# Expert layer of a decoder step: the gate product in two fp32r products, its batches over 24 slots a tile, and the samples' V rows as the moving operand

## The chip, the cores and the metric

The kernel runs on one core of one Trainium2 chip. The metric is the device time of one execution in microseconds. The kernel before takes 4426.57 us (median of 3 runs, 4424.93 to 4427.05).

## The reference

One inference step of a two-layer decoder trunk, for 512 prompt tokens and 8 sample tokens (520 together), model width 1024. Layer 0 mixes a recurrence and a latent attention, layer 1 is a convolution module. Each is followed by the same kind of expert layer, which is what the change touches:

```
q = (xb @ w_q).reshape(blk, 8, 2, 128)
s = einsum('thpd,phkd->thpk', q, sub_keys)            # 8 heads, 2 halves, 128 keys
sv, si = top_k(s, 16)                                 # per half
top_s, top_pos = top_k(all sums of the two halves, 16)
idx = i * 128 + j of the 16 picks                     # 128 x 128 experts
g = softmax(top_s)
act = gelu(einsum('thkd,td->thk', u_tab[idx], xb))
y = einsum('thk,thkd->td', g * act, v_tab[idx])
```

All of it is f32. So each token has 128 picks (8 heads of 16), each with an expert number (i, j) and a gate g, and the output is the sum of the picked rows of V, weighed by g times the GELU of the token's product with the picked row of U.

## The kernel before

The expert layer (`peer_experts`) does not gather for the prompt tokens: it computes the product of all tokens with all 16384 rows of U and lets the gates, which are zero but for the picks, choose. It does so in 128 blocks of 128 experts.

*First half, 128 slots.* In slot n TensorE forms block n of the hidden values (`hidden`, lines 1571 to 1581): x and U are each split into a rounded high part and a remainder in fp32r (a 4-byte type that TensorE multiplies in one product), and three products (low by high, high by low, high by high) over 8 chunks and two halves of 260 tokens make 48 matmuls. ScalarE rounds a loaded block to its high part (`high`, three blocks ahead) and applies the GELU of a finished block; VectorE subtracts to get the remainder (`low`, three blocks ahead); SyncE loads U five blocks ahead and stores the hidden values to memory. Every engine works its list strictly in the written order.

Into the same slots other work is laid. In slots 0 to 15 the scores and the top 16 of each half are found. Then VectorE makes the picks of one tile of 128 tokens (`select`, lines 1830 to 1897) in 13 pieces, numbered 0 to 12, of which some lie in the slots behind that slot's `low`. There are five tiles: four of the prompt, and one that holds the 8 samples, whose picks are made first. When a tile's picks are complete, TensorE transposes them (`turn_picks`, line 1583), VectorE copies them out of PSUM (line 1942), and 16 batches of 8 tokens follow, one in each slot after the tile's first four: a tile has 20 slots. For a batch VectorE makes `onej` and `onei`, 128 picks by 8 tokens by 128 numbers, by comparison of the pick's numbers with a row 0 to 127, and then multiplies `onei` by the gate (`one_hot`, lines 1922 to 1930). TensorE multiplies the two per token, in f32 (`gates`, lines 1589 to 1597), which gives the 128 x 128 map of that token's gates; ScalarE copies the maps from PSUM (`copy_gates`, line 1690), and SyncE stores 32 tokens' maps in four pieces of 512 KB, one a slot. The slots are counted by `FIND` = 16, `ONES` = 32 and `TAIL` = 112: sixteen plain slots stand before the four tiles and sixteen after them. In the code the tiles are a loop that each engine runs by itself, on VectorE three times round and a last one written out.

*Second half, 128 blocks.* The hidden values and gates come back from memory, VectorE multiplies and splits them (`gate`), and TensorE multiplies with the blocks of V, again in three fp32r products (`out`, 24 matmuls of 512 tokens).

*The samples.* Their 128 picked rows of V each are gathered (GpSimd, lines 1532 to 1536). At the very end TensorE takes, for each of 8 samples and 8 chunks of 128 outputs, 128 x 128 of V's rows as the weights and the sample's one column of gate times activation as the moving operand (lines 1656 to 1663); VectorE adds the residual (line 1995). A LayerNorm (`layer_norm`) follows, whose first matmuls are line 322 and second line 328.

What releases what in a slot: ScalarE does the batch's two `copy_gates`, then `high`, then the GELU; `high` of three blocks ahead also waits for the block before; VectorE's `low` waits for `high`; a slot's `select` pieces stand behind its `low`; the next `one_hot` stands behind them.

Of the kernel before, what the change touches and what calls it, by code (L numbers as in the profile page):

```python
# [28 lines left out]
P = 128  # L29
# [33 lines left out]
FIND, PLAIN, BATCHES = 16, 4, TT // BT  # L63
PER_TILE = PLAIN + BATCHES
ONES = FIND + 2 * BT
# [1211 lines left out]
def peer_experts(nc, k, a, layer, xh, r):  # L1277
# [7 lines left out]
    with Stage(nc, f"experts{layer}") as s:  # L1285
# [16 lines left out]
        cols = s.sb("cols", [P, 3, TT])  # L1302
        scols = s.sb("scols", [P, 3, TS])
# [5 lines left out]
        sact = s.sb("sact", [P, TS])  # L1309
# [9 lines left out]
        over = Overlay(nc, s, "over_a", 16384)  # L1319
        first = over.row()  # L1320
        onej = first.sb("onej", [P, 2, BT, NK])
        onei = first.sb("onei", [P, 2, BT, NK])
        then = over.row()
        gated = then.sb("gated", [P, TP])
        ah = then.sb("ah", [P, 2, TP], F32R)
        al = then.sb("al", [P, 2, TP], F32R)

        over = Overlay(nc, s, "over_b", 33280)
# [5 lines left out]
        rest = first.sb("rest", [TT, NT, NK])  # L1334
        top = first.sb("top", [TT, NT, TOPK])
        topi = first.sb("topi", [TT, NT, TOPK], U32)
# [3 lines left out]

        slab = k.ring
        wq = a["peer_wq"][layer]
        hidden_of = [k.ps[:, 2 * b:2 * b + 2, 0:TH] for b in range(2)]
        q_of, y_of = k.ps[:, 4:6, 0:TH], k.ps[:, 4, 0:KC * TS]
# [31 lines left out]
        cols_copied = s.sem("cols_copied")  # L1376
        one_made = s.sem("one_made")
# [8 lines left out]
        sact_ready = s.sem("sact_ready")  # L1386
        y_summed = s.sem("y_summed")
        bank_read = s.sem("bank_read")
# [7 lines left out]
        with s.block() as block:  # L1396
            @block.sync
            def _(sp):
# [66 lines left out]

                with sp.Fori(FIND // 4, ONES // 4) as i:
                    for b in range(4):
                        plain(4 * i + b, b)
                for b in range(4):
                    plain(ONES + b, b)  # L1470
                with sp.Fori(0, NP) as t:
                    first = ONES + PER_TILE * t + PLAIN
                    for v in range(PT):
                        for b in range(PT):
                            plain(first + PT * v + b, b)
                            if v:
                                store_gates(PT * t + v - 1, (v - 1) % 2, b)
                    for b in range(PT):
                        plain(first + BATCHES + b, b)
                        store_gates(PT * t + PT - 1, (PT - 1) % 2, b)  # L1480
                for n in range(TAIL + PLAIN, NK):
# [5 lines left out]
                    if n == TAIL + PLAIN:  # L1487
                        for b in range(2):
                            sp.wait_ge(g_stored[b], 16 * 4 * NQ // 2 + 64)
                    c = n - TAIL - PLAIN  # L1490
                    if c < 8:
                        load_gates(c // 4, c // 4, c % 4)
# [55 lines left out]
            def _(pe):  # L1548
# [40 lines left out]
                def gates(n, b):  # L1589

                    pe.wait_ge(one_ready, n + 1)
# [21 lines left out]
                with pe.Fori(FIND // 4, ONES // 4 - 2) as i:  # L1613
                    for b in range(4):
                        hidden(4 * i + b, b)
                turn_picks(0)
                for n in range(ONES - 8, ONES):
                    hidden(n, n)
                with pe.Fori(0, NP) as t:
                    first = ONES + PER_TILE * t  # L1620
                    for b in range(PLAIN - 1):
                        hidden(first + b, b)
                    turn_picks(t + 1)
                    hidden(first + PLAIN - 1, PLAIN - 1)
# [41 lines left out]
            def _(act_e):  # L1666
# [66 lines left out]
                for n in range(FIND, ONES):  # L1733
                    high(n + LOW, n + LOW)
                    gelu(n, n)
                    if n == FIND + 4:
                        exponentials(0)
# [489 lines left out]
```

## Time and profile before

| | before |
|---|---|
| median of 3 runs | 4426.57 us |
| the profiled execution | 4427.57 us |
| its span | 4425.5 us |
| TensorE matmul busy | 4175.6 us (94%) |
| VectorE busy | 2527.9 us (57%) |
| ScalarE busy | 1179.3 us (27%) |
| DMA, mean | 147 GB/s |

The profile is of one execution. Busy time is the share in which at least one instruction of an engine was under way. TensorE's matmuls overlap each other in the record (each is shown longer than the interval at which the next starts), so that intervals are read from start to start. An f32 matmul appears as two records, each with a weight load of its own; an fp32r matmul as one. Line numbers are those of the kernel before.

### The profile page before, as it was taken

What the parts mean: (1) busy time and instruction counts of PE and PEld (TensorE: products, weight loads), DVE (VectorE), ACT (ScalarE), POOL (GpSimd) and SP (SyncE); (2) the same over time, 40 slices, a digit from 0 to 9 for tenths busy, and PEclk for the clock granted to TensorE, in tenths of its full rate; (3) what the DMA queues carried; (4) which work ended last, traced back from release to release, by engine and by line L of the source; (5) the groups of instructions that cost most, each with busy time, mean ns of one, the idle gap of its engine ahead of it and who ended that gap; (6) DMA issues with size and microseconds to landing.
All of it is one profiled execution on the core that took longest, in us unless ns stands there. A gap on an engine that the chain in (4) does not pass through costs nothing. (4 is left out here: it accounts for less than half of the span.)

```text
span 4425.5 us, 74733 instructions
## 1 busy us (share of the span) xinstructions
PE 4175.6 (94%) x27369; PEld 3762.6 (85%) x27369; DVE 2527.9 (57%) x4678; ACT 1179.3 (27%) x1585; POOL 38.2 (1%) x43
## 2 busy tenths in 40 slices
PE   8778679999999999999998988999999999999998
PEld 8654479999999998888888567999999998888887
DVE  3742247777776435555544846787777525555553
ACT  2101132233333321121113443223333322111111
POOL 0000000000000010000000000000000001000000
PEclk9868789999999999999998989999999999999998
DMA  3026523335445565555532012334454466555551
GB/s 111 19 92 202 170 84 105 112 126 185 154 160 171 186 233 193 193 193 194 189 112 71 24 38 96 107 123 142 165 181 157 166 209 218 192 195 190 196 190 53
DMA packets 321925, 652.38 MB, mean 147 GB/s; under 512 B 26241, under 2 KB 157442, under 8 KB 321154
## 3 DMA queue, kind: packets, MB, share of 16 engines
q1 hardware_dynamic: 318978, 642.36, 43.1%
q0 software_dynamic: 2816, 8.40, 0.5%
q8 instruction: 67, 1.10, 0.1%
q14 instruction: 64, 0.52, 0.0%
HBM read 509.00 MB, written 141.53 MB: 147 GB/s over the span
## 5 line engine op out<-in xcount | busy, mean ns | idle before, releaser
L1781 DVE TENSOR_TENSOR experts_ul<-experts_u,experts_uh 128x1024 fp32r<-128x1024 f32 x512 | 627.1, 1225 | 1074.4 <-ACT experts_uh L1678 1068.0
L1578 PE MATMUL ps<-peer_x_then_r_xh,experts_ul 128*128 128x260 f32 x4096 | 1173.3, 286 | 0.0
L1579 PE MATMUL ps<-experts_over_x_xl,experts_uh 128*128 128x260 f32 x4096 | 1157.4, 283 | 0.0
L1580 PE MATMUL ps<-peer_x_then_r_xh,experts_uh 128*128 128x260 f32 x4096 | 1155.8, 282 | 0.0
L1678 ACT ACTIVATE experts_uh<-experts_u 128x1024 fp32r<-128x1024 f32 x512 | 540.8, 1057 | 1094.7 <-PE ps L1642 1085.2
L1641 PE MATMUL ps<-experts_over_a_al,experts_uh 128*128 128x512 f32 x2048 | 797.3, 389 | 0.0
L1642 PE MATMUL ps<-experts_over_a_ah,experts_uh 128*128 128x512 f32 x2048 | 797.3, 389 | 0.0
L1640 PE MATMUL ps<-experts_over_a_ah,experts_ul 128*128 128x512 f32 x2048 | 797.2, 389 | 0.0
L1579 PEld LDWEIGHTS ps<-experts_over_x_xl,experts_uh 128*128 128x128 f32 x4096 | 772.9, 189 | 0.0
L1578 PEld LDWEIGHTS ps<-peer_x_then_r_xh,experts_ul 128*128 128x128 f32 x4096 | 772.1, 189 | 0.0
L1580 PEld LDWEIGHTS ps<-peer_x_then_r_xh,experts_uh 128*128 128x128 f32 x4096 | 771.9, 188 | 0.0
L1642 PEld LDWEIGHTS ps<-experts_over_a_ah,experts_uh 128*128 128x128 f32 x2048 | 384.6, 188 | 79.7
L1641 PEld LDWEIGHTS ps<-experts_over_a_al,experts_uh 128*128 128x128 f32 x2048 | 384.5, 188 | 79.6
L1640 PEld LDWEIGHTS ps<-experts_over_a_ah,experts_ul 128*128 128x128 f32 x2048 | 384.5, 188 | 79.5
L1683 ACT ACTIVATE experts_act<-ps 128x520 f32<-128x520 f32 x256 | 154.8, 605 | 1004.7 <-PE ps L1580 1004.6
L1595 PE MATMUL ps<-experts_over_a_onei,experts_over_a_onej 128*128 128x128 f32 x2048 | 250.1, 275 | 9.7 <-DVE experts_over_a_onei L1930 9.7
L1595 PEld LDWEIGHTS ps<-experts_over_a_onei,experts_over_a_onej 128*128 128x128 f32 x2048 | 239.6, 192 | 11.3 <-issue 11.3
L1971 DVE TENSOR_TENSOR experts_over_a_al<-experts_over_a_gated,experts_over_a_ah 128x512 fp32r<-128x512 f32 x256 | 177.3, 693 | 22.2
L1558 PE MATMUL ps<-peer_x_then_r_xh,experts_over_b_slab_l 128*128 128x260 f32 x512 | 148.4, 290 | 40.8 <-DVE experts_over_x_xl L1788 34.1
L1695 ACT ACTIVATE experts_over_b_g<-ps 128x512 f32<-128x512 f32 x256 | 150.7, 598 | 122.5 <-PE ps L1595 72.0
L1965 DVE TENSOR_TENSOR experts_over_a_gated<-experts_act,experts_over_b_g 128x512 f32<-128x512 f32 x256 | 175.1, 684 | 0.5
L1930 DVE TENSOR_TENSOR experts_over_a_onei<-experts_over_a_onei,experts_cols 128x1024 f32<-128x1024 f32 x128 | 156.9, 1226 | 11.1
(342 smaller groups left out, 4770.0 us busy)
## 6 DMA issues: line engine op xcount, KB each, us to landing
experts_u<-peer_u SPq DMA_DIRECT2D x256, 512.0 KB, 3.3
experts_u<-peer_v SPq DMA_DIRECT2D x256, 512.0 KB, 3.3
hidden<-experts_act SPq DMA_DIRECT2D x256, 260.0 KB, 2.2
gates<-experts_over_b_g SPq DMA_DIRECT2D x128, 512.0 KB, 3.0
experts_over_b_g<-gates SPq DMA_DIRECT2D x128, 512.0 KB, 5.0
experts_act<-hidden SPq DMA_DIRECT2D x256, 256.0 KB, 3.6
mla_ct<-cache SPq DMA_DIRECT2D x64, 320.0 KB, 3.8
pa_ct<-cache SPq DMA_DIRECT2D x64, 320.0 KB, 3.8
```

The source lines that it names most:

```text
L1578: pe.matmul(o, ul[:, b % 4, c], xh[:, c, t], start=(c == 0), stop=False)
L1579: pe.matmul(o, uh[:, b % 4, c], xl[:, c, t], start=False, stop=False)
L1580: mm = pe.matmul(o, uh[:, b % 4, c], xh[:, c, t], start=False, stop=(c == KC - 1))
L1595: mm = pe.matmul(k.ps[:, 4 + m, e * NK:(e + 1) * NK], onej[:, b % 2, 4 * m + e], onei[:, b % 2, 4 * m + e], start=True, stop=True)
L1640: pe.matmul(k.ps[:, c, :], ul[:, b % 4, c], ah[:, b % 2], start=first, stop=False)
L1641: pe.matmul(k.ps[:, c, :], uh[:, b % 4, c], al[:, b % 2], start=False, stop=False)
L1642: mm = pe.matmul(k.ps[:, c, :], uh[:, b % 4, c], ah[:, b % 2], start=False, stop=last)
L1678: act_e.activation(uh[:, b % 4], u[:, b % 2], ACT.Copy).then_inc(high_done, 1)
L1781: v.tensor_tensor(ul[:, b % 4], u[:, b % 2], uh[:, b % 4].bitcast(F32), ALU.subtract).then_inc(split_done, 1)
L1930: v.tensor_tensor(onei[:, b % 2], onei[:, b % 2], bc(cols[:, 2, tok], 2, NK), ALU.mult).then_inc(one_ready, 1)
L1965: v.tensor_tensor(gated[:].rearrange("p (q t) -> p q t", q=NQ), act[:, b % 4, 0:TP].rearrange("p (q t) -> p q t", q=NQ), gg[:, par, :, b], ...
L1971: v.tensor_tensor(al[:, b % 2], gated[:], ah[:, b % 2].bitcast(F32), ALU.subtract).then_inc(a_ready, 1)
```

## The change

Both expert layers change in the same way.

The gate product: `onei` is single, and two further vector instructions make `one_h` and `one_l`, `onei` times the gate's rounded high part and times its remainder, as fp32r. TensorE's one f32 matmul per token becomes two fp32r matmuls that accumulate. A tile takes 24 slots instead of 20, with no plain slots ahead: two of each three slots have a batch. The pieces of `select` go, two at a time, into the slots in which VectorE makes no batch. The prompt's first tile is chosen first and the samples' last, so that 8 instead of 16 slots stand before the tiles (`ONES` = 24, `TAIL` = 120), and 8 behind. The four stores of 32 tokens' maps are issued together at the end of each six slots. The VectorE loop goes round all four tiles, each with a full set of pieces.

The samples: the picked V rows become the moving operand, 512 columns wide, and the weights are 32 columns of which the first is the sample's. Four samples go to the four groups of 32 columns of the array. Two samples' halves make 4 PSUM banks; ScalarE and VectorE copy two banks each, 16 transposes follow, and four vector instructions add the residual.

```diff
-FIND, PLAIN, BATCHES = 16, 4, TT // BT
-PER_TILE = PLAIN + BATCHES
-ONES = FIND + 2 * BT
+FIND, BATCHES = 16, TT // BT
+PER_TILE = BATCHES * 3 // 2
+ONES = FIND + 8
...
 (SyncE)
+                    for b in range(PER_TILE):
+                        plain(first + b, b)
+                        if b % 6 == 5:
+                            for c in range(4):
+                                store_gates(PT * t + b // 6, b // 6 % 2, c)
...
 (TensorE, gates)
-                            mm = pe.matmul(k.ps[:, 4 + m, e * NK:(e + 1) * NK], onej[:, b % 2, 4 * m + e], onei[:, b % 2, 4 * m + e],
-                                           start=True, stop=True)
+                            pe.matmul(o, onej[:, b % 2, at], one_h[:, b % 2, at], start=True, stop=False)
+                            mm = pe.matmul(o, onej[:, b % 2, at], one_l[:, b % 2, at], start=False, stop=True)
...
 (TensorE, tiles)
+                    turn_picks(t)
+                    with pe.Fori(0, 2) as v:
+                        for b in range(PER_TILE // 2):
+                            if b % 3:
+                                a_ = b - 1 - b // 3
+                                gates(BATCHES * t + BATCHES // 2 * v + a_, a_)
+                            hidden(first + PER_TILE // 2 * v + b, b)
...
 (ScalarE, tiles)
+                        if b % 3:
+                            a_ = b - 1 - b // 3
+                            copy_gates(BATCHES * t + a_, a_, v)
                         plain(first + b, b)
+                        if b == 10:
+                            exponentials(t + 1)
...
 (VectorE)
+                    v.tensor_tensor(onej[:, b % 2], bc(k.iota[:], 1, BT), bc(cols[:, 1, tok], 2, NK), ALU.is_equal)
+                    wait(v, one_ready, n + 1)
+                    v.tensor_tensor(onei[:], bc(k.iota[:], 1, BT), bc(cols[:, 0, tok], 2, NK), ALU.is_equal).then_inc(one_made, 1)
+                    wait(v, one_made, n + 1)
+                    v.tensor_tensor(one_h[:, b % 2], onei[:], bc(gate_h[:, tok].bitcast(F32), 2, NK), ALU.mult)
+                    v.tensor_tensor(one_l[:, b % 2], onei[:], bc(cols[:, 2, tok], 2, NK), ALU.mult).then_inc(one_ready, 1)
+
+                PIECES = {2: (0, 1), 5: (2, 3), 8: (4, 5), 11: (6, 7), 14: (8, 9), 17: (10, 11), 20: (12,)}
+
+                with v.Fori(0, NP) as t:
+                    v.wait_ge(turned, t + 1)
+                    v.tensor_copy(cols[:], turn).then_inc(cols_copied, 1)
+                    wait(v, cols_copied, t + 1)
+                    v.tensor_copy(gate_h[:], cols[:, 2]).then_inc(gate_ready, 1)
+                    wait(v, gate_ready, 2 * t + 1)
+                    v.tensor_tensor(cols[:, 2], cols[:, 2], gate_h[:].bitcast(F32), ALU.subtract).then_inc(gate_ready, 1)
+                    wait(v, gate_ready, 2 * t + 2)
+                    for b in range(PER_TILE):
+                        if (b + 1) % 3:
+                            a_ = b - b // 3
+                            one_hot(BATCHES * t + a_, BT * a_, a_)
+                        low(first + b + LOW, b + LOW)
+                        for piece in PIECES.get(b, ()):
+                            select(piece, t + 1, t + 1, chain, STEPS * (t + 1))
...
 (TensorE, samples)
-                pe.wait_ge(bank_read, 1)
-                for n in range(TS):
-                    for c in range(KC):
-                        mm = pe.matmul(y_of[:, c * TS + n:c * TS + n + 1], rows[:, n, c * P:(c + 1) * P], sact[:, n:n + 1],
-                                       start=True, stop=True)
+                pe.wait_ge(bank_read, 4)
+                for b in range(4):
+                    for g in range(4):
+                        n, half = b // 2 * 4 + g, slice(b % 2 * 512, b % 2 * 512 + 512)
+                        mm = pe.matmul(k.ps[g * 32:(g + 1) * 32, 4 + b, :], sact[:, n], rows[:, n, half], start=True, stop=True)
+                    mm.then_inc(y_summed, 1)
+                pe.wait_ge(bank_read, 8)
+                for b in range(4):
+                    if b % 2 == 0:
+                        pe.wait_ge(y_copied[b // 2], 1)
+                    for c in range(4):
+                        mm = pe.transpose(k.ps[:, b, c * P:(c + 1) * P], y_row[:, b, c * P:(c + 1) * P], k.ident[:])
...
 (ScalarE, VectorE, samples)
+                act_e.activation(y_row[:, 0:2], k.ps[:, 4:6, :], ACT.Copy).then_inc(y_copied[0], 1)
+                v.tensor_copy(y_row[:, 2:4], k.ps[:, 6:8, :]).then_inc(y_copied[1], 1)
+                v.wait_ge(y_turned, 1)
+                for b in range(4):
+                    cs, ts = slice(b % 2 * 4, b % 2 * 4 + 4), slice(TP + b // 2 * 4, TP + b // 2 * 4 + 4)
+                    v.scalar_tensor_tensor(r[:, cs, ts], k.x[:, cs, ts], ALPHA, y_turn[:, b, :, :, 0], ALU.mult, ALU.add)
```

## Rows read from the trace of the kernel before

**Rows 1.** Windows: layer 0's tiles. Stretch, its length, busy us per engine, clock, DMA

```profile
955.00:1467.00 512.00, 507.17 (x4290) 506.37 (x4289) 366.68 (x473) 184.41 (x265) 0.00 (x0) 1.00 0.47 161
```

**Rows 2.** Waits of TensorE: who, for whom, us in total, times, longest

```profile
PE ps L1595 <- DVE experts_over_a_onei L1930: 9.7, 8, 1.3
```

**Rows 3.** Timeline of TensorE, one slot with a batch: start us, duration us

```profile
1113.30 1.95 PE L1595 MATMUL ps<-experts_over_a_onei,experts_over_a_onej 128*128 128x128 f32 x16
1115.01 0.37 PE L1578 MATMUL ps<-peer_x_then_r_xh,experts_ul 128*128 128x260 f32 x1
1115.21 0.29 PE L1579 MATMUL ps<-experts_over_x_xl,experts_uh 128*128 128x260 f32 x1
...
1120.84 1.95 PE L1595 MATMUL ps<-experts_over_a_onei,experts_over_a_onej 128*128 128x128 f32 x16
```

**Rows 4.** Windows of line 1661 alone: PE busy, PEld busy, granted clock, DMA

```profile
2306.00:2310.00 4.00, 4.00 (x38) 4.00 (x38) 1.00 0.00 0
2320.00:2325.00 5.00, 5.00 (x25) 5.00 (x25) 0.50 0.00 0
```

**Rows 5.** Groups by line: the weight loads of the fp32r and f32 products

```profile
L1579 PEld LDWEIGHTS ps<-experts_over_x_xl,experts_uh 128*128 128x128 f32 x4096 | 772.9, 189 | 0.0
L1595 PEld LDWEIGHTS ps<-experts_over_a_onei,experts_over_a_onej 128*128 128x128 f32 x2048 | 239.6, 192 | 11.3 <-issue 11.3
```

**Rows 6.** Timeline, all engines, start of a tile's first batch

```profile
1101.10 0.55 DVE L1942 COPY experts_cols<-ps 128x384 f32<-128x384 f32 x1
...
1101.84 1.22 DVE L1926 TENSOR_TENSOR experts_over_a_onej<-iota,experts_cols 128x1024 f32<-128x1024 f32 x1 [0.20 <-DVE experts_cols L1942]
...
1102.98 1.22 DVE L1927 TENSOR_TENSOR experts_over_a_onei<-iota,experts_cols 128x1024 f32<-128x1024 f32 x1
...
1105.66 2.05 PE L1595 MATMUL ps<-experts_over_a_onei,experts_over_a_onej 128*128 128x128 f32 x16 [1.28 <-DVE experts_over_a_onei L1930]
```

**Rows 7.** Timeline of VectorE: `low` in the slot of rows 3

```profile
1116.87 1.23 DVE L1781 TENSOR_TENSOR experts_ul<-experts_u,experts_uh 128x1024 fp32r<-128x1024 f32 x1 [1.01 <-ACT experts_uh L1678]
```

**Rows 8.** Timeline of VectorE: loop's return, then pieces of `select`

```profile
1084.30 1.23 DVE L1781 TENSOR_TENSOR experts_ul<-experts_u,experts_uh 128x1024 fp32r<-128x1024 f32 x1 [3.05 <-issue]
1086.90 0.69 DVE L1845 TENSOR_TENSOR experts_cand<-experts_over_x_values 128x512 f32 x1 [1.38 <-issue]
...
1089.85 1.23 DVE L1781 TENSOR_TENSOR experts_ul<-experts_u,experts_uh 128x1024 fp32r<-128x1024 f32 x1 [0.18 <-DVE experts_best L1850]
...
1092.77 0.26 DVE L1855 MATCH_REPLACE8 experts_crest<-experts_best,experts_cand 128x112 f32<-128x112 f32 x1
...
1110.47 1.50 DVE L1859 MAX8 experts_best<-experts_crest 128x8 f32<-128x112 f32 x8
...
1118.01 0.09 DVE L1863 MATCH_VALUE_LOAD experts_pos<-experts_best,experts_crest 128x8 f32 x1
...
1120.38 1.22 DVE L1926 TENSOR_TENSOR experts_over_a_onej<-iota,experts_cols 128x1024 f32<-128x1024 f32 x1
...
1155.71 2.28 DVE L1838 TENSOR_TENSOR experts_pick<-experts_ra,iota 128x2048 f32<-128x2048 f32 x1
1158.18 1.22 DVE L1926 TENSOR_TENSOR experts_over_a_onej<-iota,experts_cols 128x1024 f32<-128x1024 f32 x1 [0.18 <-DVE experts_pick L1838]
```

**Rows 9.** Timeline of TensorE in the attention: a run of column-grouped f32 products

```profile
380.47 1.93 PE L994 MATMUL ps<-mla_ct,layer_wide 128*32 128x256 f32 x32
```

**Rows 10.** Groups by line, whole span: samples' product, LayerNorm's matmuls, transposes

```profile
L1661 PE MATMUL ps<-experts_sact,experts_over_x_rows 128*128 128x1 f32 x256 | 47.1, 322 | 0.0
L328 PE MATMUL ps<-ln_sq,mean_d 128*128 128x260 f32 x128 | 28.7, 383 | 0.0
L322 PE MATMUL ps<-peer_x_then_r_r,mean_d 128*128 128x260 f32 x64 | 19.3, 474 | 2.6 <-PEq L128 2.6
L1586 PE MATMUL ps<-ident,experts_ijg 128*128 128x128 f32 x30 | 4.9, 272 | 0.0
```

**Rows 11.** Timeline of VectorE: the samples' residual in layer 1

```profile
4387.51 0.22 DVE L1995 SCALAR_TENSOR_TENSOR peer_x_then_r_r<-x,ps 128x64 f32<-128x64 f32 x1 [23.82 <-PE ps L1661]
```

More of the change, by code:

```diff
@@ L1386, in peer_experts @@
         sact_ready = s.sem("sact_ready")
+        sact_cleared = s.sem("sact_cleared")
         y_summed = s.sem("y_summed")
+        y_copied = [s.sem(f"y_copied{b}") for b in range(2)]
+        y_turned = s.sem("y_turned")
         bank_read = s.sem("bank_read")
@@ L1464, in plain @@
                     store(n, b)
[L1466 to L1470, printed above, removed]
-                with sp.Fori(0, NP) as t:
[L1472 to L1481, printed above, removed]
+                for n in range(FIND, ONES):
+                    plain(n, n)
+                with sp.Fori(0, NP) as t:
+                    first = ONES + PER_TILE * t
+                    for b in range(PER_TILE):
[3 more added lines that the diff above has]
+                                store_gates(PT * t + b // 6, b // 6 % 2, c)
+                for n in range(TAIL, NK):
                     if n + LOAD < NK:
@@ L1612, in _ @@
                     hidden(b, b)
[L1613 to L1617, printed above, removed]
+                for n in range(FIND, ONES):
                     hidden(n, n)
@@ L1620, in _ @@
                     first = ONES + PER_TILE * t
[L1621 to L1624, printed above, removed]
-                    with pe.Fori(0, BATCHES // 4) as v:
-                        for b in range(4):
-                            gates(BATCHES * t + 4 * v + b, b)
-                            hidden(first + PLAIN + 4 * v + b, b)
+                    turn_picks(t)
[5 more added lines that the diff above has]
+                            hidden(first + PER_TILE // 2 * v + b, b)
+                turn_picks(NP)
                 for n in range(TAIL, NK):
@@ L1731, in exponentials @@
                     act_e.activation(expd[:], expd[:], ACT.Exp).then_inc(exped, 1)
[L1733 to L1737, printed above, removed]
-                    if n == FIND + 12:
-                        exponentials(1)
                 def plain(n, b):
@@ L1743, in plain @@
                     gelu(n, b)
[L1745 to L1760 removed]
+                for n in range(FIND, ONES):
+                    plain(n, n)
+                    if n == FIND + 4:
+                        exponentials(0)
+                with act_e.Fori(0, NP) as t:
+                    first = ONES + PER_TILE * t
+                    for b in range(PER_TILE):
+                        v = b // 6
+                        if b % 6 == 1:
+                            act_e.wait_ge(g_stored[v % 2], 64 * (2 * t + v // 2) + 64)
+                        if b % 3:
+                            a_ = b - 1 - b // 3
+                            copy_gates(BATCHES * t + a_, a_, v)
+                        plain(first + b, b)
+                        if b == 10:
+                            exponentials(t + 1)
                 for n in range(TAIL, NK):
@@ L1784, in _ @@
                 v.sem_inc(score_free, 1)
+                v.sem_inc(one_ready, 1)
                 slab_low(0, 0)
```

102 lines of the change are left out of this document (37 added, 65 removed).

## The prediction

> **What bounds the kernel now.** I read the windows first. In layer 0's tiles the matmul engine is busy 507 of 512 us at full granted clock, VectorE 367, ScalarE 184, and the DMA engines are 0.47 busy [rows 1]. So TensorE sets the pace, and what a change of it saves there comes out at the end one for one. The waits come second: TensorE waits for the batches' one-hot arrays 9.7 us in 8 times, once at the start of each of 8 tiles, about 1.2 us each, and nowhere else in a tile [rows 2]. Third the timeline of a slot, for what a batch costs: 16 records from 1113.30 to 1115.01, 1.71 us, 0.107 us each; the first hidden matmul behind them takes 0.20 us, and the other 47 take 5.63, 0.120 each; the slot is 7.54 us [rows 3]. A plain slot is thus 48 x 0.120 = 5.75. Last the end of a layer, where TensorE works alone: the samples' product takes 47.1 us in both layers, 23.6 each, with nothing beside it [rows 10, 11].
>
> **The gate product.** 16 f32 records of 128 columns become 16 fp32r matmuls of 128 columns. No fp32r matmul narrower than 260 columns is in the trace, so the price is bounded. The streaming of 128 columns at 2.4 GHz is 0.053, and the 260-column product shows 0.120 for 0.108, 0.012 over its stream: 0.065 if only the stream counts. But each product brings a weight load. The fp32r load's record is as long as the f32 one's, 189 against 192 ns [rows 5], and what a row of loads costs with hardly a stream behind it is seen in the samples' product of one column: 38 records in 4 us at full clock, 0.105, and 25 in 5 us at half clock, 0.200, which halves to 0.100 [rows 4]. I take 0.100. The batch is then 1.60, and the 0.08 of the first hidden matmul (change of type) goes: slot 7.35, 0.19 less, x 128 batches = **-24 us** (0.105 would make it -14). Upper ends: 0.120, if the interval of the 260-column product is that of its loads: 16 x 0.120 + 5.75 = 7.67, +17; and four cycles a column, the f32 rate, 0.213: 16 x 0.213 + 5.75 = 9.16, +207.
>
> The Trainium skill (TensorE: Matmul & The Clock Gate, Weight-path perf modes) says that weights load four chunks at once where there are 128 of them and the type is not FP32, with no gain for fp32. The rows speak for the FP32 side: equal load records. By the fast side the product would cost its stream alone, which is the first rival below. The same page (Back-to-back issue gap) gives about 81 ns a product for pairs of load and 128 columns; by that the batch is 1.30 and the term -62 instead of -24. No row here shows it.
>
> **VectorE's extra product and the order of its work.** 128 more instructions of 1.14 us from start to start [rows 6] are 146 us of work. VectorE has 145 us idle per layer in the tiles [rows 1], so by busy time they cost nothing. But it works in order, and the pieces now stand two at a time behind a `low` that is released late. Take a slot with a batch that starts at S on TensorE, of the kind whose VectorE part has pieces (b = 2, 5, 8, ...). `low` began at S + 3.57 there [rows 3, 7]: GELU, the batch's two copies and `high` go before it on ScalarE. The next instruction starts 1.14 later, S + 4.7, and S + 4.6 with the shorter batch. Then come the pieces, P, and only then the `one_hot` that the slot after next needs: 3.82 us from its start to TensorE's [rows 6] plus one more instruction, 4.96. It is ready at S + 9.6 + P. TensorE is there at S + 1.60 + 2 x 5.75 = S + 13.1. It waits P - 3.5.
>
> The pieces, start to next start [rows 8]: piece 0 2.95 (1086.90 to 1089.85); pieces 1 and 2 2.0 each (1090.99, which is 1089.85 + 1.14, to 1093.03); piece 3 1.7 (1.50 and a semaphore); piece 4 2.37; pieces 7 to 11 2.47 each (1155.71 to 1158.18 shows one); pieces 5 and 6 have eight and four small instructions and are put at 1.9 and 1.3, estimates under piece 4; piece 12, one wide and three short, 3.2. The pairs: 4.95, 3.7, 4.3, 3.8, 4.94, 4.94, and 3.2 alone. Waits 1.45, 0.2, 0.8, 0.3, 1.45, 1.45, 0: 5.6 us a tile, x 8 = **+45 us**. Before, single pieces stood between batches and no such wait is in [rows 2]. Nothing absorbs it: once late, TensorE's later slots are late too, and VectorE gets ahead again only by the next group of three. The second batch of a group has slack (ready 1.14 + 4.96 = 6.1 after the first, needed after 7.35).
>
> **The start of a tile.** The three transposes now stand one slot before the first batch. From the copy of the picks to TensorE's start were 4.56 us [rows 6]; two short instructions with their semaphores (about 0.9, an estimate from the 0.74 between the copy and the next) and the extra product make it 6.6, and with about 0.6 for transposes and their landing the batch is ready 7.2 behind the first transpose, TensorE 0.3 + 5.75: a wait of 1.1, as the 1.2 before. The loop's return is new there: VectorE stood 3.05 us after it and 1.38 again after its first instruction, both put down to issue [rows 8]. The first part lies in VectorE's idle time (its `low` ends at S + 4.7, the slot at S + 7.35); the second falls into the chain: 3 returns x 2 layers x 1.4 = **+9 us** (0 to 27).
>
> Four stores at once and gates' first loads in 8 slots instead of 16: covered by U being loaded five blocks ahead and the DMA engines being half idle; without that cover 2 MB at the 161 GB/s of [rows 1] are 13 us a layer, up to +26. ScalarE's work per slot falls. I take 0.
>
> **The samples.** New: 16 f32 products of 512 columns, 32 records. Column-grouped f32 products of 256 columns ran 32 records in 1.93 us [rows 9], 0.060 each where 256 columns by [rows 3] would be 0.214 one after the other. So 32 records of 512 take 3.9, and 0.3 to land; VectorE's copy of 1024 columns about 1.3 (a 1024-column pass is 1.22 [rows 6]); the first eight transposes lie under it, the second eight cost 8 x 4.9 / 30 = 1.3 [rows 10]; four short vector instructions at 0.22 [rows 11] 0.9. In all 7.7 against 23.6 + 0.2: 16.1 x 2 = **-32 us**. If the groups did not overlap: 32 x 0.428 = 13.7 instead of 3.9, and -13. The first LayerNorm matmuls behind take 19.3 / 2 = 9.65 us where the same number at line 328 takes 28.7 / 4 = 7.2 [rows 10], because the clock fell to half in the one-column product [rows 4]. With full-width streams it may stay up: 0 to -5; I take **-2**.
>
> **Sum.** -24 + 45 + 9 - 32 - 2 = -4 us against the profiled execution of 4427.6: 4423.6. The median shown is 1.0 below that execution: 4422.6. I say 4422.
>
> **Rivals.**
> 1. *The fp32r product costs its stream only*, 0.065: batch 1.04, slot 6.79, -96 instead of -24; the waits grow a little (+8, ScalarE's copies bind). Total -68: 4358. For it: the array has nothing else to do; against it: [rows 4, 5].
> 2. *No wait behind the pairs*: VectorE's busy time is under 85% of a tile (24 x 1.14 + 16 x 4.8 + 30 + 3 = 137 of 164 us). Then -49: 4377. Against it: the order above leaves VectorE idle first and late afterwards.
> 3. *Slower: the load sets 0.120 a product.* Then the product gains nothing, +17 instead of -24, and the waits outweigh the samples' gain: +37: 4464. For it: 260 columns take 0.012 over their stream, and loads stand between all of them. It decides from about 0.107 a product (16 x 0.107 gives a term of -10 and a total of +10).
> 4. *Narrow fp32r at the f32 rate*: +207 instead of -24, +227: 4654. No row for it, none excludes it.
> 5. *The column groups don't overlap* (other weights and sources than in [rows 9]): +15: 4441.
>
> **Chances.** Forecast 0.52; rival 1 0.14; rival 2 0.11; rival 3 0.12; rival 4 0.06; rival 5 0.05. A measurement tells 0.2%, 9 us, from no change. Within the forecast the load (0.100 or 0.105: 10 us), the returns (0 to 27), pieces 5 and 6, and the LayerNorm's clock make 4400 to 4445, which leaves 0.17 faster, 0.22 same and 0.13 slower. Rivals 1 and 2 are faster (0.25), rivals 3 to 5 slower (0.23, with 0.03 of it same at their near ends). Faster 0.42, same 0.25, slower 0.33. The range takes in rivals 2, 3 and 5 and leaves out 1 and 4: 4368 to 4466.
>
> **What would show it.** The interval of the gate product, start to start: 0.100, or 0.065, or 0.120. TensorE waiting for the last `one_hot` product about 56 times (7 a tile) rather than 8, with about 1.4 us behind pairs (0,1), (8,9) and (10,11) and nearly none behind 12. First batches of tiles 1 to 3 waiting about 2.5. From the last V block to the samples' residual under 9 us. It is wrong if TensorE's waits in the tiles stay near 10 us in all, or if the product is outside 0.095 to 0.11.

## The result, and the profile after

The changed kernel takes 4476.25 us (median of 4 runs, 4473.70 to 4484.80), the kernel before beside it 4425.75 us (4 runs, 4423.59 to 4427.05). The ratio is 1.0115, with a 95% interval of 1.0102 to 1.0128: slower by 50 us. The forecast was 4422 us and its range ended at 4466.

The profiled execution took 4473.7 us, with a span of 4471.9, 46.4 more than the kernel before's 4425.5. The head of the page after, and its groups by line of the second half of a layer (the product of the gated activations with the V blocks) and of the gate product. Columns: busy us, mean ns of one, idle time before and who ended it.

```profile
span 4471.9 us, 75067 instructions
PE 4182.7 (94%) x27209; PEld 3715.9 (83%) x27209; DVE 2675.4 (60%) x4832; ACT 1182.5 (26%) x1587; POOL 39.1 (1%) x43
...
L1641 PE MATMUL ps<-experts_over_a_ah,experts_uh 128*128 128x512 f32 x2048 | 810.0, 396 | 0.0
L1639 PE MATMUL ps<-experts_over_a_ah,experts_ul 128*128 128x512 f32 x2048 | 810.0, 395 | 0.0
L1640 PE MATMUL ps<-experts_over_a_al,experts_uh 128*128 128x512 f32 x2048 | 810.0, 395 | 0.0
...
L1599 PE MATMUL ps<-experts_over_a_one_h,experts_over_a_onej 128*128 128x128 f32 x1024 | 234.4, 275 | 42.1 <-DVE experts_over_a_one_l L1924 42.1
L1599 PEld LDWEIGHTS ps<-experts_over_a_one_h,experts_over_a_onej 128*128 128x128 f32 x1024 | 196.0, 191 | 53.5 <-issue 53.5
```

The windows of layer 0's tiles and the waits of TensorE answer to [rows 1, 2]:

```profile
955.00:1467.00 512.00, 496.21 (x4151) 491.93 (x4150) 386.24 (x530) 173.58 (x245) 0.00 (x0) 1.00 0.49 157
```

```profile
PE ps L1599 <- DVE experts_over_a_one_l L1924: 42.1, 48, 1.3
```

TensorE is 11 us less busy in these 512, at the same full clock, and VectorE 20 us busier. The waits for the one-hot arrays went from 9.7 us in 8 times to 42.1 in 48.

The timeline of TensorE, one batch with its wait, answers to [rows 3] (start us, duration us):

```profile
963.00 0.28 PE L1583 MATMUL ps<-peer_x_then_r_xh,experts_uh 128*128 128x260 f32 x1
963.69 0.32 PE L1599 MATMUL ps<-experts_over_a_one_h,experts_over_a_onej 128*128 128x128 f32 x1 [0.41 <-DVE experts_over_a_one_l L1924]
963.85 0.28 PE L1600 MATMUL ps<-experts_over_a_one_l,experts_over_a_onej 128*128 128x128 f32 x1
963.96 0.27 PE L1599 MATMUL ps<-experts_over_a_one_h,experts_over_a_onej 128*128 128x128 f32 x1
...
965.41 0.28 PE L1600 MATMUL ps<-experts_over_a_one_l,experts_over_a_onej 128*128 128x128 f32 x1
965.52 0.33 PE L1581 MATMUL ps<-peer_x_then_r_xh,experts_ul 128*128 128x260 f32 x1
965.70 0.28 PE L1582 MATMUL ps<-experts_over_x_xl,experts_uh 128*128 128x260 f32 x1
```

The products start 0.112 us apart (the mean of all is 0.1117), not 0.100. The batch takes 1.83 us here, and its first product 0.16 (963.69 to 963.85). Of the 128 batches the 56 behind a gap, short ones counted, take 1.83 each; the other 72 take 1.73, with a first interval of 0.06. The first hidden matmul behind a batch takes 0.17 us in the mean (0.18 here) instead of 0.12, where the kernel before had 0.20 [rows 3].

The start of the samples' part in layer 1, all engines, answers to [rows 4, 10, 11]:

```profile
4429.62 3.64 PE L1661 MATMUL ps<-experts_over_x_rows,experts_over_a_sact 128*32 128x512 f32 x32
...
4431.67 1.02 ACT L1771 ACTIVATE experts_u<-ps 128x1024 f32<-128x1024 f32 x1 [23.23 <-PE ps L1661]
...
4433.33 1.23 DVE L1996 COPY experts_u<-ps 128x1024 f32<-128x1024 f32 x1 [2.92 <-PE ps L1661]
...
4434.61 1.09 PE L1668 MATMUL ps<-ident,experts_u 128*128 128x128 f32 x8 [0.33 <-DVE experts_u L1996]
4435.74 0.41 DVE L2000 SCALAR_TENSOR_TENSOR peer_x_then_r_r<-x,ps 128x16 f32<-128x16 f32 x4 [1.18 <-PE ps L1668]
...
4437.22 6.87 PEld L322 LDWEIGHTS ps<-peer_x_then_r_r,mean_d 128*128 128x128 f32 x32 [1.76 <-issue]
```

From the first row's start to the end of the four residual instructions it takes 6.5 us, where 7.7 were forecast. The LayerNorm's sums behind it take about 7, as they do at full clock.

Where the time of the span went, from start to start of TensorE's records:

| | before | after | difference, us |
|---|---|---|---|
| idle before batches, all 128 | 10.9 | 50.9 | +40 |
| the batches, 128 times | 1.709 | 1.778 | +9 |
| first hidden matmul behind a batch | 0.203 | 0.173 | -4 |
| the other hidden products | 119.85 ns | 119.81 ns | -1 with what lies between |
| second half, 6144 products of 512 columns | 226.68 ns | 233.33 ns | **+41** |
| samples' first product to the LayerNorm's 32nd, 2 layers | 33.3 + 34.9 | 14.5 + 14.5 | -39 |

(The waits here count the short ones too, which the page of the profile leaves out.) The sum is +46, as is the span's difference. The largest row is one that the prediction does not have: the diff has no line in the second half's product. Its records, before and after, start to start:

```profile
2099.69 0.39 PE L1641 MATMUL ps<-experts_over_a_al,experts_uh 128*128 128x512 f32 x1
2099.91 0.39 PE L1642 MATMUL ps<-experts_over_a_ah,experts_uh 128*128 128x512 f32 x1
2100.14 0.39 PE L1640 MATMUL ps<-experts_over_a_ah,experts_ul 128*128 128x512 f32 x1
2100.37 0.39 PE L1641 MATMUL ps<-experts_over_a_al,experts_uh 128*128 128x512 f32 x1
2100.59 0.39 PE L1642 MATMUL ps<-experts_over_a_ah,experts_uh 128*128 128x512 f32 x1
```

```profile
2099.63 0.40 PE L1639 MATMUL ps<-experts_over_a_ah,experts_ul 128*128 128x512 f32 x1
2099.87 0.40 PE L1640 MATMUL ps<-experts_over_a_al,experts_uh 128*128 128x512 f32 x1
2100.10 0.40 PE L1641 MATMUL ps<-experts_over_a_ah,experts_uh 128*128 128x512 f32 x1
2100.33 0.40 PE L1639 MATMUL ps<-experts_over_a_ah,experts_ul 128*128 128x512 f32 x1
2100.56 0.40 PE L1640 MATMUL ps<-experts_over_a_al,experts_uh 128*128 128x512 f32 x1
```

The group of L1640 before, whose counterpart after is L1639 above:

```profile
L1640 PE MATMUL ps<-experts_over_a_ah,experts_ul 128*128 128x512 f32 x2048 | 797.2, 389 | 0.0
```

Four intervals are 0.90 us before and 0.93 after. Weights, blocks, shapes and clock are the same. What differs is the place of `ah` and `al` in SBUF: the samples' new `sact` (1024 bytes a partition) lies ahead of them, the old one (32 bytes) is gone, and `gate_h` (512) is new. In the built programs `ah` starts at byte 169152 of the partition before, a multiple of 64, and at byte 170656 after, 32 past one. `al` lies 4096 bytes behind it in both.

### The profile page after: what moved, and what is told of

Same layout as the page of the kernel before. It is cut to its first block and busy times, and to the rows that moved or that the text cites. A ratio compares the mean times of both kernels' runs of the same rounds, so it can differ in the third digit from the quotient of the medians.

```text
span 4471.9 us, 75067 instructions
## 1 busy us (share of the span) xinstructions
PE 4182.7 (94%) x27209; PEld 3715.9 (83%) x27209; DVE 2675.4 (60%) x4832; ACT 1182.5 (26%) x1587; POOL 39.1 (1%) x43
## 5 line engine op out<-in xcount | busy, mean ns | idle before, releaser
L1641 PE MATMUL ps<-experts_over_a_ah,experts_uh 128*128 128x512 f32 x2048 | 810.0, 396 | 0.0
L1639 PE MATMUL ps<-experts_over_a_ah,experts_ul 128*128 128x512 f32 x2048 | 810.0, 395 | 0.0
L1640 PE MATMUL ps<-experts_over_a_al,experts_uh 128*128 128x512 f32 x2048 | 810.0, 395 | 0.0
L1640 PEld LDWEIGHTS ps<-experts_over_a_al,experts_uh 128*128 128x128 f32 x2048 | 384.7, 188 | 93.0
L1639 PEld LDWEIGHTS ps<-experts_over_a_ah,experts_ul 128*128 128x128 f32 x2048 | 384.7, 188 | 93.0
L1599 PE MATMUL ps<-experts_over_a_one_h,experts_over_a_onej 128*128 128x128 f32 x1024 | 234.4, 275 | 42.1 <-DVE experts_over_a_one_l L1924 42.1
L1599 PEld LDWEIGHTS ps<-experts_over_a_one_h,experts_over_a_onej 128*128 128x128 f32 x1024 | 196.0, 191 | 53.5 <-issue 53.5
L1600 PE MATMUL ps<-experts_over_a_one_l,experts_over_a_onej 128*128 128x128 f32 x1024 | 235.1, 274 | 0.0
L1600 PEld LDWEIGHTS ps<-experts_over_a_one_l,experts_over_a_onej 128*128 128x128 f32 x1024 | 196.2, 192 | 0.0
```

The lines of the kernel that those rows point to most:

```text
L1599: pe.matmul(o, onej[:, b % 2, at], one_h[:, b % 2, at], start=True, stop=False)
L1600: mm = pe.matmul(o, onej[:, b % 2, at], one_l[:, b % 2, at], start=False, stop=True)
L1639: pe.matmul(k.ps[:, c, :], ul[:, b % 4, c], ah[:, b % 2], start=first, stop=False)
L1640: pe.matmul(k.ps[:, c, :], uh[:, b % 4, c], al[:, b % 2], start=False, stop=False)
L1641: mm = pe.matmul(k.ps[:, c, :], uh[:, b % 4, c], ah[:, b % 2], start=False, stop=last)
```

## The experiments

Each ran beside the kernel before on the same chip, and ratios are to it. There were three chips: one for experiments 1 and 2, one for 3 to 5, one for 6. The kernel before had medians of 4427.4, 4428.9 and 4427.8 us there, so that a difference between experiments of different chips is good to a microsecond or two.

**1. The place of ah alone, in the kernel before** (b_ah32: 32 bytes ahead; b_ah1536: 1536 bytes, still a multiple of 64) **and in the changed kernel** (a_ah32).

```diff
 b_ah32
         gated = then.sb("gated", [P, TP])
+        then.sb("pad", [P, 8])
         ah = then.sb("ah", [P, 2, TP], F32R)
 b_ah1536
+        then.sb("pad", [P, 384])
 a_ah32
         sact = then.sb("sact", [P, TS, P // 4])
+        then.sb("pad", [P, 8])
         ah = then.sb("ah", [P, 2, TP], F32R)
```

> The kernel before with 32 bytes of padding ahead of ah and al (the moving operand of the second half), so that they start at 32 instead of 0 modulo 64 bytes, as in the changed kernel; nothing else moves. Theory A (the start of the moving operand modulo 64 bytes sets the interval of a 512-column fp32r product): the interval goes from 226.7 to 233.3 ns, 6144 products x 6.6 ns = +41 us, about 4467. Theory B (something else of the changed kernel's second half: the gates' array, the store pattern, the order of transfers): interval stays 226.7, time stays 4426.

> The kernel before with 1536 bytes of padding ahead of ah and al, so that they lie elsewhere but still at 0 modulo 64 bytes. Theory A: no change, 4426 and 226.7 ns. Theory C (the place of the moving operand relative to the weights matters, not its start modulo 64): the interval rises, up to 4467.

> The changed kernel with 32 bytes of padding ahead of ah and al alone, so that they start at 0 modulo 64 bytes again. Theory A: the interval of the second half falls from 233.3 to 226.7 ns, 4476 - 41 = 4435. Theory B: no change, 4476. The waits of the first half (6.4 us a tile) stay in both.

| | median, us (runs) | ratio, 95% | interval of 512 columns |
|---|---|---|---|
| b_ah32 | 4468.80 (4) | 1.0095, 1.0078 to 1.0112 | 233.33 ns |
| b_ah1536 | 4428.06 (10) | 1.0002, 0.9993 to 1.0012 | 226.68 ns |
| a_ah32 | 4436.34 (10) | 1.0022, 1.0013 to 1.0032 | 226.68 ns |

The group of b_ah32 and then that of a_ah32:

```profile
L1641 PE MATMUL ps<-experts_over_a_ah,experts_ul 128*128 128x512 f32 x2048 | 809.5, 395 | 0.0
```

```profile
L1640 PE MATMUL ps<-experts_over_a_ah,experts_ul 128*128 128x512 f32 x2048 | 796.7, 389 | 0.0
```

32 unused bytes make the kernel before 41 us slower, and 32 unused bytes take 40 us off the changed one; nothing else moves (the waits and the batches keep their numbers in both). A move of 1536 bytes costs nothing, so distance alone is not the cause. The size of the step is less sure than it looks: every start that ran at 226.68 ns is the same not only within 64 bytes but within 512 (the moves were 0, 1024 and 1536 bytes), and both that ran at 233.33 are 32 bytes off such a start. "A multiple of 64" is what fits below; 128, 256 or 512 would fit as well. In all the experiments that follow, `ah` has a start that ran fast, so that those on the changed kernel are compared with a_ah32.

**2. The samples' part alone, in the kernel before.** The old `sact`'s 32 bytes stay as padding and the new one lies behind `al`.

```diff
-        sact = s.sb("sact", [P, TS])
+        pad = s.sb("pad", [P, TS])
...
         al = then.sb("al", [P, 2, TP], F32R)
+        sact = then.sb("sact", [P, TS, P // 4])
...  (and the products, copies, transposes and residual of the change)
```

> The kernel before with the samples' part of the change alone (V rows stream past 32-column weights, copies, transposes); the new weights lie behind al, and the old ones' 32 bytes stay as padding, so that every other array keeps its place. If the two parts of the change add up: -19 and -20 us from the end of the last V block to the LayerNorm's first sums, 4426 - 39 = 4387. If the samples' part brought the slower second half with it: 4387 + 41 = 4428.

4386.29 us (4 runs, 4384.64 to 4388.20), ratio 0.9908 (0.9892 to 0.9925): 41 us faster, with the second half at 226.68 ns. It is the part of the change that does more than was forecast for it (-34).

**3. The order of VectorE's work.** In a_ah32, the pieces go ahead of the slot's `low`.

```diff
-                        low(first + b + LOW, b + LOW)
                         for piece in PIECES.get(b, ()):
                             select(piece, t + 1, t + 1, chain, STEPS * (t + 1))
+                        low(first + b + LOW, b + LOW)
```

> The changed kernel with ah and al back at 0 modulo 64 bytes (as a_ah32, 4436), and in VectorE's list the pieces of select ahead of the slot's low instead of behind it; the same instructions. Theory (the pieces stand behind a low that is released late): VectorE does them while it would wait for ScalarE, the batch behind is ready at about S + 11 and TensorE comes at S + 13: the waits behind pieces go (5.5 us a tile, 44 in all), 4392. Rival (VectorE is short of time in a tile, not badly ordered): its busy time is the same, so the waits stay, 4436.

4386.30 us (4 runs), ratio 0.9902 (0.9886 to 0.9919), 50 us less than a_ah32. First VectorE in the changed kernel, around the pieces of tile 0's slot 11, then in this one, then this one's waits:

```profile
969.34 1.22 DVE L1783 TENSOR_TENSOR experts_ul<-experts_u,experts_uh 128x1024 fp32r<-128x1024 f32 x1
975.71 1.23 DVE L1783 TENSOR_TENSOR experts_ul<-experts_u,experts_uh 128x1024 fp32r<-128x1024 f32 x1 [5.14 <-ACT experts_uh L1684]
976.85 0.29 DVE L1880 TENSOR_TENSOR experts_ra<-experts_ra,experts_is_b 128x128 f32<-128x128 f32 x1
...
978.04 2.30 DVE L1841 TENSOR_TENSOR experts_pick<-experts_ra,iota 128x2048 f32<-128x2048 f32 x1
980.52 1.23 DVE L1919 TENSOR_TENSOR experts_over_a_onej<-iota,experts_cols 128x1024 fp32r<-128x1024 f32 x1 [0.18 <-DVE experts_pick L1841]
...
984.13 1.22 DVE L1924 TENSOR_TENSOR experts_over_a_one_l<-experts_over_a_onei,experts_cols 128x1024 fp32r<-128x1024 f32 x1
```

```profile
967.33 2.29 DVE L1842 TENSOR_TENSOR experts_pick<-experts_ra,iota 128x2048 f32<-128x2048 f32 x1
...
973.39 1.23 DVE L1784 TENSOR_TENSOR experts_ul<-experts_u,experts_uh 128x1024 fp32r<-128x1024 f32 x1 [3.78 <-ACT experts_uh L1685]
974.54 1.22 DVE L1920 TENSOR_TENSOR experts_over_a_onej<-iota,experts_cols 128x1024 fp32r<-128x1024 f32 x1
```

```profile
PE ps L1600 <- DVE experts_over_a_one_l L1925: 5.9, 8, 0.7
```

In the changed kernel VectorE stands 5.14 us for ScalarE's high part and does the pieces afterwards, with the next batch's arrays behind them. With the pieces first they lie in that idle time, and the arrays follow `low` at once. The waits fall from 50.9 to 7.2 us, all at the tiles' first batches; the work is the same to the instruction. The batch's mean falls from 1.778 to 1.740, since 120 of the 128 now follow without a gap and take 1.73: that is another 5 us, which a wait costs beyond itself (0.10 each, 48 times).

**4. The type of the gate product.** In a_ah32, back to the f32 product of the kernel before, with three vector instructions a batch. The slots are those of the change, and the pieces stay behind `low`.

```diff
-                            pe.matmul(o, onej[:, b % 2, at], one_h[:, b % 2, at], start=True, stop=False)
-                            mm = pe.matmul(o, onej[:, b % 2, at], one_l[:, b % 2, at], start=False, stop=True)
+                            mm = pe.matmul(o, onej[:, b % 2, at], onei[:, b % 2, at], start=True, stop=True)
...
-                    v.tensor_tensor(one_h[:, b % 2], onei[:], bc(gate_h[:, tok].bitcast(F32), 2, NK), ALU.mult)
-                    v.tensor_tensor(one_l[:, b % 2], onei[:], bc(cols[:, 2, tok], 2, NK), ALU.mult).then_inc(one_ready, 1)
+                    v.tensor_tensor(onei[:, b % 2], onei[:, b % 2], bc(cols[:, 2, tok], 2, NK), ALU.mult).then_inc(one_ready, 1)
```

> The changed kernel with ah and al at 0 modulo 64 bytes, the new order of slots and pieces, but the gate product of before: one f32 product per token, three vector instructions a batch. The batch on TensorE 1.71 instead of 1.78 us (-9), and the waits behind pieces become P - 3.5 - 1.14: about 0.3 three times a tile or less, so -38. In all 4436 - 47 = 4389. If the order alone makes the waits, they stay near 5 us a tile: 4427.

4384.39 us (4 runs), ratio 0.9898 (0.9882 to 0.9915), 52 us less than a_ah32. The batch's mean is 1.721 us against 1.778, and the waits are 5.8 us in all, in an order of work that had 50.9 with the fourth instruction. The page of the profile, without the short ones:

```profile
PE ps L1598 <- DVE experts_over_a_onei L1920: 2.0, 9, 0.4
```

The split buys TensorE nothing. From a batch's start to the second hidden matmul behind it, where no gap stands ahead, both forms take 1.906 us: 1.703 and 0.203 in f32 (the kernel before, best1), 1.734 and 0.172 in fp32r (the changed kernel, a_pieces1st), and inside a batch the records start 0.1116 us apart in all four. The 1.14 us that the split adds to VectorE's part of each batch is what makes that order late. So either of two edits, this one or the one of 3, takes the same waits away.

**5. What sets the fp32r product's interval.** In a_ah32, a_mov64 streams 64 of the 128 moving columns, a_w64 loads 64 of the 128 weight columns. Each leaves out half of every token's map.

```diff
 a_mov64
-                            o, at = k.ps[:, 4 + m, e * NK:(e + 1) * NK], 4 * m + e
+                            o, at = k.ps[:, 4 + m, e * NK:e * NK + 64], 4 * m + e
-                            pe.matmul(o, onej[:, b % 2, at], one_h[:, b % 2, at], start=True, stop=False)
+                            pe.matmul(o, onej[:, b % 2, at], one_h[:, b % 2, at, 0:64], start=True, stop=False)
 a_w64
+                            o, at = k.ps[0:64, 4 + m, e * NK:(e + 1) * NK], 4 * m + e
+                            pe.matmul(o, onej[:, b % 2, at, 0:64], one_h[:, b % 2, at], start=True, stop=False)
...  (the product with one_l likewise)
```

> As a_ah32, but the two fp32r gate products take 64 of the 128 moving columns (the other half of each token's map is left out). Read from the trace: the interval between gate products. If the weight load sets it, it stays at 0.111 us; if the stream does (128 columns are 0.053), it falls by 0.027 to about 0.085.

> As a_ah32, but the weights of the two gate products are 64 of the 128 columns (half of each token's map is left out), with all 128 moving columns. If the weight load sets the interval, it falls from 0.111 to about half, 0.055 to 0.065 us; if it is the stream or a fixed cost of the product, it stays.

Each ran once. Groups of a_mov64, then of a_w64:

```profile
L1600 PE MATMUL ps<-experts_over_a_one_h,experts_over_a_onej 128*128 128x64 f32 x1024 | 231.1, 272 | 40.8 <-DVE experts_over_a_one_l L1925 40.8
L1600 PEld LDWEIGHTS ps<-experts_over_a_one_h,experts_over_a_onej 128*128 128x128 f32 x1024 | 196.5, 192 | 51.9 <-issue 51.9
...
L1582 PE MATMUL ps<-peer_x_then_r_xh,experts_ul 128*128 128x260 f32 x4096 | 1187.3, 290 | 0.0
```

```profile
L1600 PE MATMUL ps<-experts_over_a_one_h,experts_over_a_onej 128*64 128x128 f32 x1024 | 138.4, 224 | 49.7 <-DVE experts_over_a_one_l L1925 48.9
L1600 PEld LDWEIGHTS ps<-experts_over_a_one_h,experts_over_a_onej 128*64 128x64 f32 x1024 | 125.4, 135 | 61.1 <-issue 61.1
```

Half the stream leaves the interval as it is (median 0.112 us), half the load takes it to 0.060 and the batch from 1.78 to 0.98. So the load sets it: 0.112 for 128 columns. a_w64 took 4334.88 us, 101 less than a_ah32, and 128 batches of 0.80 less are 102. a_mov64 took 4465.76, 29 *more* than a_ah32 (on another chip), though it does less. The windows of the tiles say where, a_ah32 ahead of a_mov64:

```profile
955.00:1467.00 512.00, 496.21 (x4151) 491.93 (x4150) 386.27 (x534) 173.02 (x244) 0.00 (x0) 1.00 0.49 157
```

```profile
955.00:1467.00 512.00, 496.70 (x4067) 492.68 (x4066) 376.33 (x509) 170.09 (x239) 0.00 (x0) 0.98 0.48 152
```

TensorE does 84 records less in the same time at a granted clock of 0.98 instead of 1.00, and the hidden products have a mean of 290 ns instead of 284. From start to start the 12118 intervals between hidden products sum to 1502 us where a_ah32 has 1462; 527 of them are over 0.16 us, as at half clock, where a_ah32 has 170. That is the 29 us and more. Only this one run shows it, and whether it would come again is not known.

**6. What the parts make together.** best1: the changed kernel with the f32 product, the pieces first, and every array on a multiple of 64 bytes. best2 also starts the moving operands of the hidden products on such multiples, with rows of 528 columns, split 256 and 264, where rows of 520 (2080 bytes) split in two have starts of 0, 16, 32 and 48 past one.

```diff
 best1 (against the changed kernel; the f32 product as in 4, the order as in 3)
-        gate_h = s.sb("gate_h", [P, TT], F32R)
+        s.sb("pad", [P, 8])
-        over = Overlay(nc, s, "over_a", 4 * 7 * BT * NK)
+        over = Overlay(nc, s, "over_a", 16384)
 best2 (against best1)
-        xh = over.row().sb("xh", [P, KC, T], F32R)
+        xh = over.row().sb("xh", [P, KC, 528], F32R)
-                        o, t = hidden_of[b % 2][:, h], slice(h * TH, (h + 1) * TH)
+                        t = slice(256 * h, 256 if h == 0 else T)
...  (xl likewise; GELU in two instructions)
```

> The samples' part of the change, the new order of slots with the pieces ahead of the slot's low, the f32 gate product of before, and all arrays at 0 modulo 64 bytes as in the kernel before. From a_f32 (4384): its waits of 5.7 us go, the batch stays at 1.71 to 1.72 us: 4379. Against a_pieces1st (4386), which has the same order with the fp32r product, the difference should be the batch (0.02 to 0.07 us x 128 = 3 to 9) and nothing else. If the fp32r product were worth something on its own, a_pieces1st would be the faster one.

> As best1, and the first half's moving operands also start at 0 modulo 64 bytes: rows of xh and xl are 528 instead of 520 elements apart, and the two products per chunk take 256 and 264 tokens instead of 260 and 260 (in best1 they start at 0, 16, 32 or 48 modulo 64). The GELU becomes two instructions. If the 6.6 ns that 512 columns cost at 32 modulo 64 holds in proportion for 260, the interval falls from 119.8 by up to 3.4 ns: 12288 products, -42 us, 4337. If the first half is set by something else than the moving operand's read (its interval is near the 0.111 us of a weight load), nothing changes: 4379.

best1: 4377.20 us (4 runs, 4376.49 to 4378.21), ratio 0.9887 (0.9871 to 0.9904). best2: 4374.53 (4 runs, 4373.80 to 4375.69), ratio 0.9882 (0.9866 to 0.9899). The windows of best1's tiles:

```profile
955.00:1467.00 512.00, 512.00 (x4328) 512.00 (x4328) 346.01 (x493) 179.89 (x253) 0.00 (x0) 1.00 0.48 163
```

TensorE never stands: 512 of 512. It waits before no batch, which neither order had reached with four vector instructions a batch. best2's gain is 2.7 us, with hidden intervals of 119.66 ns for 119.86; so starts off a multiple of 64, which cost 6.65 ns at 512 columns, have no such price at 260. best1 is 9 us under a_pieces1st, which is that one's 7 us of waits and what they cost behind them; the type itself adds nothing (experiment 4).

## Why the prediction was wrong

It failed in one step that was missing and in one that was mis-sized; the two other large terms came out near their numbers.

*The step that is missing: the second half of a layer was taken as unchanged.* No sentence of the prediction asks where the arrays come to lie that follow the new ones in SBUF. That is +41 of the +50 us, and shown from both sides (b_ah32, a_ah32, and b_ah1536 against a rival by distance). The rows at hand could not price it, but the diff shows the shift: +1024 + 512 - 32 bytes is 1504, not a multiple of 64.

*The step that was mis-sized: the fp32r gate product at 0.100 us, forecast -24, measured 0.* (The table's +9 for the batches and -4 for the matmul behind them leave +5, which is what 48 more gaps cost the batches behind them, at 0.10 each as in experiment 3.) The load was the right cause and its price was misread. [rows 4] count the records that a window touches, also those that only reach into it, and each is longer than its interval: 38 in 4 us gave 0.105, and 25 in 5 us at half clock gave 0.200 and by halving 0.100. From start to start the same records of the kernel before are 0.1117 apart at full clock and 0.213 at half. The second misreading hid the first: the f32 batch was put at 0.107 a record [rows 3], which is 1.71 us over 16, but its records start 0.1116 apart too, and the first hidden matmul starts only 0.03 after the last of them. With 0.1117 in the prediction's own sum the slot is 16 x 0.1117 + 5.75 = 7.54, no change, as measured. So the answer lay in the trace of the kernel before. The sign that the prediction gave for being wrong here, a product outside 0.095 to 0.11, came true by a little.

Rival 3's price of 0.120 was too high, and its +37 for the total came out nearest by luck, since the slower second half made up the rest; its mechanism, a load that sets the product and takes all of its gain, is what a_w64 and a_mov64 show, and 0.112 lies past the 0.107 from which it decides. Rival 1 (0.065) falls, and so does rival 4: the narrow fp32r product of 128 columns takes 0.112, not 0.213.

The surcharge of 0.08 on the first hidden matmul behind a batch had been put down to the change of type. It stays at 0.05 with the same type on both sides, so the type explains the 0.03 between at most, and inside the batch that is lost again (1.906 us to the second hidden matmul either way).

The Trainium skill (TensorE: Matmul & The Clock Gate, Back-to-back issue gap) has about 81 ns for a pair of load and 128 columns. The fp32r pairs here measure 112, and the measurement decides.

*VectorE's order, forecast +45, measured +40, and +45 with what a gap costs the batch behind it.* This was the right reading, and the count came out too: TensorE waits 56 times, 7 a tile, short waits counted. The gaps of one tile (us):

| the batch | forecast | measured |
|---|---|---|
| tile's first | 1.1 | 0.90 |
| behind pieces 0, 1 | 1.45 | 1.44 |
| 2, 3 | 0.2 | 0.17 |
| 4, 5 | 0.8 | 0.56 |
| 6, 7 | 0.3 | 0.87 |
| 8, 9 | 1.45 | 1.18 |
| 10, 11 | 1.45 | 1.27 |
| 12 | 0 | 0 |

The wait behind pieces 6 and 7 is the one that is off, and experiment 3's rows of the changed kernel show it: `low` begins 4.38 us behind the batch at 971.33, not 3.57. ScalarE in that slot:

```profile
971.52 0.60 ACT L1689 ACTIVATE experts_act<-ps 128x520 f32<-128x520 f32 x1 [4.26 <-PE ps L1583]
972.15 1.28 ACT L1737 ACT_TABLE_LOAD   x1
973.44 0.31 ACT L1737 ACTIVATE experts_expd<-experts_expd 128x128 f32<-128x128 f32 x1
973.66 1.07 ACT L1701 ACTIVATE experts_over_b_g<-ps 128x512 f32<-128x512 f32 x2
974.61 1.06 ACT L1684 ACTIVATE experts_uh<-experts_u 128x1024 fp32r<-128x1024 f32 x1
```

The exponentials of the next tile, with a table load of 1.28 us, stand ahead of the copies and of the high part that `low` waits for. The step had left them out. That the order is the cause is shown by a_pieces1st. Rival 2, no wait because VectorE has idle time, falls: it has 126 us of it in the 512, and TensorE waits all the same.

*The loop's return, forecast +9, measured 0.* The gaps above are the same in every tile, the first included, so no return reaches TensorE. Behind a return VectorE stands 3.3 us until the transposes are done, and 0.9 where no return is ahead; the return lies in that wait, so the chain for which it was priced does not run through VectorE. Whether the 1.38 us of [rows 8] are part of it the trace does not tell.

*The samples, forecast -34 with the LayerNorm's clock, measured -39, and -41 alone.* The column groups do overlap, which settles rival 5: 32 records in 3.64 us where 3.9 were taken, and the sums behind them go at full clock (a mean of 385 ns, where the same line had 474 [rows 10]).

By the terms as measured, 0 + 45 + 0 - 39 + 41 = +47. Without the shift of `ah` it would have been about +6; a_ah32 is +8.9 over the kernel before in the same runs (4436.34 against 4427.42). The forecast had -4. About 10 us of its error are terms that it had, and that it is so little is partly luck, because they offset each other: +24 from the product, -9 from the return, -5 from the samples. The other 41 are the one that it had not.

## What to carry to other kernels

When an edit adds, drops or resizes an SBUF array, work out by how much each array behind it moves, above all wide moving operands that the edit does not name, and keep the start that it had within 64 bytes (within 512 to be safe, since only such moves were tried); a pad of 32 bytes here is worth 41 us. Read an interval from start to start at full clock, not as a window's length over its count of records, and compare the old form's and the new one's that way: here both small products are set by the same weight load, and the change of type could gain nothing. On an engine that works in order, work without a deadline goes ahead of the instruction that waits for another engine, not behind it.

## What the runs showed of the hardware

An fp32r moving operand of 512 columns costs 226.7 ns a product when `ah` and `al` start on a multiple of 64 bytes and 233.3 ns when they start 32 past one, with the same weights (before, b_ah1536, a_ah32 against after, b_ah32). The matmul records are longer too (395 against 389 ns). With about 260 columns, starts of 0, 16, 32 and 48 past, as they come in turn in rows of 2080 bytes, cost 0.2 ns a product in the mean (119.86 against 119.66, best1 against best2). Why the wide operand pays and the narrow one does not is open. With 512 columns a start of 16 past was not tried, nor were moves by 64, 128 or 256 bytes, which would tell the step.

Products with 128 weight columns start every 0.112 us at full clock, whether fp32r with 128 moving columns, fp32r with 64, or f32 records with 128 or with one column; at half clock the one-column records start every 0.213. With 64 weight columns the interval is 0.060.

A batch of these products takes 0.10 us more behind a gap, whether of 0.1 or of 1.4 us, than behind none, in f32 (1.803 against 1.703) and in fp32r (1.834 against 1.734), at the same full granted clock.

Fewer columns streamed went with a longer time once: in a_mov64 TensorE's granted clock was 0.97 to 0.98 in the tiles, and the run was 29 us longer than the one with twice the columns. What TensorE did before the clock fell is known only as that, and one run stands for it.
